# Gates computed between the values' projection steps, and the output gate's projection spread over the steps of the heads' chain, in a two-stage transformer kernel on one core

## The reference

```python
def odd_mixer(nc, nl, w_in, gate_b, head_g, w_out, need_ctx):
    pc = nc @ (w_in if need_ctx else w_in[:, :ML_QKVG])
    pl = nl @ w_in                       # q, k, v, gates, output gate
    qc, kc, vc, gc = mlstm_inputs(pc, gate_b)
    ql, kl, vl, gl = mlstm_inputs(pl, gate_b)
    ...                                  # scans forward and backward: h_l
    h = rmsnorm(h, head_g.reshape(ML_HEADS, ML_DV)).reshape(Bh, T, ML_MIX)
    return (jax.nn.sigmoid(p[..., ML_QKVG:]) * h) @ w_out
```

## Time and profile before

| what | us |
|---|---|
| three runs: median (lowest to highest) | 3825.74 (3823.3 to 3829.73) |
| profiled execution: its own time | 3827.59 |
| its span in the trace | 3826.3 |
| PE busy over the span | 3038.8 (79%) |
| DVE busy over the span | 2461.3 (64%) |
| ACT busy over the span | 762.1 (20%) |
| POOL busy over the span | 930.9 (24%) |

### The profile page before, as it was taken

The page is one execution under the profiler, slowest core; times in us unless marked ns, Lnnn a source line. Parts: engine busy times, 40 slices in busy tenths (PEclk is TensorE's granted clock), DMA queues, the critical chain, the costliest instruction groups (busy, mean ns, idle before and its releaser), DMA issues. The chain is left out here.

```text
span 3826.3 us, 28525 instructions
## 1 busy us (share of the span) xinstructions
PE 3038.8 (79%) x8761; PEld 1590.9 (42%) x8761; DVE 2461.3 (64%) x5376; ACT 762.1 (20%) x1854; POOL 930.9 (24%) x842
## 2 busy tenths in 40 slices
PE   6898886799997889887767778777897786778776
PEld 1354455467433468354344223222343462223222
DVE  2124357798676678745568998666514549997665
ACT  1002123224222523225311111000102211110000
POOL 0000001222322133222302434333100013435332
PEclk7899887899998899988878999999996699999999
DMA  6554334799897579966747999999632059999998
GB/s 221 190 187 152 121 113 147 296 370 351 319 377 284 211 310 414 401 241 212 290 151 281 387 389 397 422 422 421 258 138 103 17 200 357 387 386 415 422 422 341
DMA packets 205546, 1102.17 MB, mean 288 GB/s; under 512 B 23796, under 2 KB 24128, under 8 KB 107088
## 3 DMA queue, kind: packets, MB, share of 16 engines
q0 software_dynamic: 114512, 818.87, 54.0%
q1 hardware_dynamic: 90256, 280.91, 20.4%
q10 hardware_dynamic: 624, 0.57, 0.1%
HBM read 1099.18 MB, written 1.05 MB: 288 GB/s over the span
## 5 line engine op out<-in xcount | busy, mean ns | idle before, releaser
L2098 PE MATMUL PS<-AR 128*128 128x512 f32 x2456 | 1198.5, 633 | 386.1 <-DVE AR L2140 342.7
L2197 POOL DMA_INDIRECT AR<-in_uv,AR x768 | 854.2, 1112 | 1695.2 <-PE PS L2098 1159.5
L2145 DVE CUSTOM_DVE_ANT_0 AR<-AR 128x1024 f32<-128x1024 f32 x768 | 937.3, 1222 | 318.0 <-DMA AR<-in_uv,AR 316.2
L2098 PEld LDWEIGHTS PS<-AR 128*128 128x128 f32 x2456 | 469.4, 200 | 1076.2 <-DVE AR L2140 534.6
L750 PE MATMUL PS<-AR 128*128 128x512 f32 (+4 forms) x1176 | 500.5, 579 | 20.8 <-DMA AR<-in_w_in 6.5
L2110 ACT ACTIVATE AR<-AR 128x2 f32<-128x2 f32 x384 | 78.1, 203 | 1552.7 <-DVE AR L2145 1547.2
L750 PEld LDWEIGHTS PS<-AR 128*128 128x128 f32 x1176 | 222.1, 203 | 279.2 <-issue 243.6
L350 DVE SCALAR_TENSOR_TENSOR AR<-AR,CC 128x512 f32<-128x512 f32 x280 | 211.6, 756 | 184.4 <-DMA AR<-in_w_ada 105.2
L1051 PE MATMUL PS<-AR 128*128 128x256 f32 x1408 | 317.1, 384 | 10.2 <-DMA AR<-in_w_up_lin 8.8
L1051 PEld LDWEIGHTS PS<-AR 128*128 128x128 f32 x1408 | 268.9, 192 | 69.0 <-issue 18.0
L2017 PE MATMUL PS<-AR 128*128 128x256 f32 x768 | 196.3, 420 | 39.7 <-ACT AR L806 19.2
(11 more groups left out here) (226 smaller groups left out, 2578.3 us busy)
## 6 DMA issues: line engine op xcount, KB each, us to landing
AR<-in_w_mod SPq DMA_DIRECT2D x96, 512.0 KB
AR<-in_w_ada SPq DMA_DIRECT2D x160, 256.0 KB, 7.0
AR<-in_w_in SPq DMA_DIRECT2D x56, 512.0 KB
AR<-in_peer_w_q SPq DMA_DIRECT2D x48, 512.0 KB
AR<-in_w_up_act SPq DMA_DIRECT2D x44, 512.0 KB
AR<-in_w_up_lin SPq DMA_DIRECT2D x44, 512.0 KB
AR<-in_w_down SPq DMA_DIRECT2D x44, 512.0 KB
AR<-in_even_w_in SPq DMA_DIRECT2D x24, 512.0 KB
```

Source lines behind the costliest of these rows:

```text
L2098: ins = pe.eng.matmul(acc[i][hh], e.dg(x), e.buf(x)[:, 1024 + 512 * hh:1536 + 512 * hh], start=(x == e.on[False][i][0]), stop=(x == e.on[F ...
L2145: v.eng.tensor_tensor_reduce(e.buf(x)[:, 0:1024], e.buf(x)[:, 0:1024], norm2(e).H[e.tiles[x // 128]], 1.0, 0.0, ALU.mult, ALU.add, DT[x // ...
L2197: g.eng.indirect_dma_start(e.buf(x), None, D["uv"][e.l], bass.IndirectOffsetOnAxis(ap=idx_at(x // 16, x % 16, 1), axis=0)).then_inc(*land. ...
```

## The change

The order becomes `oq`, `ok`, `og`, `ov`, `oo`. In the first four, `odd_front` does two pieces of modulation after each step, and in `ov` one step of the gates as well, on each engine. The projection `oo` is no longer in the front: `odd_units` does one of its eight steps after each iteration of the heads' chain, on PE and ACT. It uses banks 0 and 1 (`GATED`) and the chain's own ring shrinks to banks 2 to 5 (`MID`). The transposes of q and k become a stage of their own, s0, one iteration ahead, so the chain has 12 iterations; the copy of k (`KTO`) moves from DVE to ACT. Since the turned activations must live until `oo` ends, the chain's tiles move from `HT8` to `SL`, behind its first 4096 columns. SP issues the same loads in the new order: two pieces of modulation behind each chunk of the first 17, then the eight chunks of `oo` alone.

```diff
-        EB = [HT8[:, 1536 + 512 * i:2048 + 512 * i] for i in range(6)]
+        EB = [SL[:, 5632 + 512 * i:6144 + 512 * i] for i in range(6)]
...
-        odd_lins = [("oq", (0, 512), [0, 1]), ("ok", (512, 1024), FOUR), ("ov", (1024, 2048), FOUR),
-                    ("og", (2048, 2064), FOUR), ("oo", (2064, 3088), [0, 1])]
+        odd_lins = [("oq", (0, 512), [0, 1]), ("ok", (512, 1024), FOUR), ("og", (2048, 2064), FOUR),
+                    ("ov", (1024, 2048), FOUR), ("oo", (2064, 3088), [0, 1])]
+        GATED, MID = (0, 1), (2, 3, 4, 5)
+
+        def odd_front(lane, steps, gates):
+
+            gates = iter(gates)
+            for n, cols, tiles in odd_lins[:-1]:
+                for _ in steps(n, cols, tiles):
+                    lane.fill(2)
+                    if n == "ov":
+                        next(gates, None)
+            lane.flush()
+            through(gates)
+
+        def odd_units(last, *parts):
+
+            for _ in stages(8, *parts):
+                next(last, None)
+            through(last)
...
+            def gates():
+                for _ in range(4):
+                    yield
+                bk = bank(pe, MAIN, "cum")
+                pe.wait_ge(("lf",), ("late",))
...
+                ins.then_inc(*pe.done("mm", "cum"))
+                yield
+                yield
+                bk = bank(pe, MAIN, "ut")
...
-                    bk = bank(pe, SIX, "ou", u, d)
+                    bk = bank(pe, MID, "ou", u, d)
...
-            skewed(8, s1, nothing, s2, s3)
+            odd_units(steps(*odd_lins[-1]), s0, s1, nothing, s2, s3)
...
+            odd_front(sp, lambda n, cols, tiles: lin(sp, 8, cols, tiles, nothing), ())
+            through(lin(sp, 8, odd_lins[-1][1], [0, 1], nothing))
...
+            def gates():
+                yield
+                a.wait_ge(a.last, ("gl",))
+                a.eng.activation(EG, LG, ACT.Exp, scale=-1.0).then_inc(*a.done("ge"))
+                yield
+                a.wait_ge(a.last, ("g1",))
+                a.eng.activation(EG, EG, ACT.Ln).then_inc(*a.done("gn"))
...
+                    copy_act(a, KTO[h % 2], psum("flip", "ok", h), ("mm", "flip", "ok", h),
+                             ("mm", "osc", u - 3)).then_inc(*a.done("ev", "flip", "ok", h))
...
-                if t == 0:
-                    copy_dve(v, KTO[h % 2], psum("flip", "ok", h), ("mm", "flip", "ok", h),
-                             ("mm", "osc", u - 3)).then_inc(*v.done("ev", "flip", "ok", h))
```

More of the change, by code:

```diff
@@ L2221, in odd_pe @@
             seen = {}
[L2222 to L2239, removed]
+            def steps(n, cols, tiles):
+                return lin_pe(pe, (n,), W3, 8, cols, tiles, ALL.tile, prep=n1, seen=seen,
+                              ring=LINES if n in ("oq", "ok") else GATED if n == "oo" else MAIN)
@@ new lines, in gates @@
+            def gates():
[3 more added lines that the diff above has]
+                pe.wait_ge(("lf",), ("late",))
+                for d, order, tri in ((0, (2, 3, 0, 1), "up"), (1, (3, 2, 1, 0), "lo")):
+                    for n, j in enumerate(order):
+                        for m in range(n + 1):
+                            ins = pe.eng.matmul(bk[:, j * 8 + d * 4:j * 8 + d * 4 + 4], cst(tri) if m == n else cst("one"),
+                                                LG[:, order[m], d * 8 + 4:d * 8 + 8], start=(m == 0), stop=(m == n))
+                ins.then_inc(*pe.done("mm", "cum"))
+                yield
+                yield
+                bk = bank(pe, MAIN, "ut")
+                pe.wait_ge(("ug",))
+                for t in FOUR:
+                    ins = pe.eng.transpose(bk[0:8, t * 128:(t + 1) * 128], UG[:, t, :], ident)
+                ins.then_inc(*pe.done("mm", "ut"))
@@ L2241, in s1, with s0 @@
+            odd_front(pe, steps, gates())
+            def s0(u):
+                h, t = units3[u]
+                if t == 0:
+                    flip_pe(pe, ("oq", h), [Qp[:, i, h * 128:(h + 1) * 128] for i in range(2)], MID,
+                            [("ev", "lin", "oq", x, 0) for x in range(2)])
+                    flip_pe(pe, ("ok", h), [Kp[:, i, h * 128:(h + 1) * 128] for i in FOUR], MID,
+                            [("ev", "lin", "ok", x, 512) for x in FOUR])
             def s1(u):
@@ L2259, in s2 @@
             def s2(u):
-                bk = bank(pe, SIX, "opt", u)
+                bk = bank(pe, MID, "opt", u)
                 pe.wait_ge(("oe", u))
@@ L2309, in odd_act, with steps, s0 @@
             seen = set()
-            for n, cols, tiles in odd_lins:
-                for _ in lin(a, 8, cols, tiles, takes[n], prep=n1, seen=seen):
-                    a.fill()
-            a.flush()
-            a.wait_ge(a.last, ("gl",))
-            a.eng.activation(EG, LG, ACT.Exp, scale=-1.0).then_inc(*a.done("ge"))
-            a.wait_ge(a.last, ("g1",))
-            a.eng.activation(EG, EG, ACT.Ln).then_inc(*a.done("gn"))
-            def s1(u):
+            def steps(n, cols, tiles):
+                return lin(a, 8, cols, tiles, takes[n], prep=n1, seen=seen)
+            def gates():
[5 more added lines that the diff above has]
+                a.eng.activation(EG, EG, ACT.Ln).then_inc(*a.done("gn"))
+            odd_front(a, steps, gates())
+            def s0(u):
                 h, t = units3[u]
@@ L2379, in odd_dve, with steps @@
[L2379 to L2386 removed]
+            def steps(n, cols, tiles):
+                return lin(v, 8, cols, tiles, nothing, prep=n1, seen=seen)
```

79 lines of the change are left out of this document (37 added, 42 removed).

## The result

The change makes the kernel faster. In the runs made beside each other, before took 3827.73 us (3823.3 to 3833.93, 4 runs) and after 3782.32 us (3775.84 to 3786.57, 4 runs): ratio 0.9882, 95% interval 0.9864 to 0.9899, 45.4 us less. The forecast was 3774 in a range of 3758 to 3796.

A forecast was written before the change was run, and what follows sets the result against it. PE bounds the front; a loop of waits, mostly at low clock, bounds the chain. First scores 40.9 us earlier plus 10.6 off the chain save 51.5: span 3774.8, forecast 3774 us, range 3758 to 3796.

The forecast's parts named there:

- The bound of the front: Front, projections before the heads' chain: PE is the limit, nearly always at full clock, busy 107.3 of 111 us.
- my 9.3: Front, within v's steps: the gates' sums 7.1 us, slow matmuls behind 1.7, transposes 0.5; together 9.3 us.
- The loads wait 3 us: Front, q's steps: three loads pass four buffers, costing PE between no wait and 8 us; taken as 3.
- DVE's two pieces (3.1 us) are too: Front, k's and v's steps: DVE's two modulation pieces, 3.1 us, are hidden behind a 7.4 us step.
- The third rival: Front held: four buffers at upper bound (+5 us), gates' round trips bare (+8), giving 3787 us; chance 9%.
- The hand-over to the chain: Front's end: PE waits about 1.8 us for v's copies, six transposes 0.82, first `oo` step 3.7.
- the 2844.98 from which I added up: Front: the old kernel's end of q, k, v and three modulation halves, 2844.98 us, used as base for added work.
- The chain: Heads' chain: 92.5 us for 103.1 with `oo` inside, about 10.0 us an iteration, mean clock over 0.8.
- The first rival: Front and chain: the low clock takes over from v's last steps, 22.5 us slower, 3848 us; chance 4%.
- The added wait: Chain, `oo`'s fifth step: PE waits 5.5 us for ACT to empty banks 0 and 1; iteration 17 us for 10.
- The k copy: Chain: k's copy leaves DVE's loop, where it held every head's first scores; gain counted within the loop's 9.0 us.
- All later stages shifted alike: After the chain: a sign that the forecast is right is that every later stage moves by the same amount.

The follow-up runs named there:

- act_late: after with, on ACT alone, one piece of modulation moved from q's last step to k's first, behind q's copies; median 3774.08 us, ratio 0.9874.
- sig_first: after with ACT's copies and Sigmoids of `oo` ahead of its part of the units within an iteration, PE's list unchanged; median 3777.8 us, ratio 0.9882.
- k_dve_late: gates_only with transposes of q and k back in the iteration that uses them and k's copy back on DVE; median 3815.36 us, ratio 0.9964.
- gates_only: after with `oo` back ahead of the chain, gates and modulation still between the front's projection steps; median 3802.47 us, ratio 0.9939.
- idle_mm: gates_only plus four matmuls of `oo`'s shape, results unread, in eight steps of the chain; median 3802.56 us, ratio 0.9934.
- q_light: after with, on all engines, one piece of modulation beside each step of q and three beside each of k; median 3771.48 us, ratio 0.986.
- both: after with the edits of q_light and sig_first together; median 3769.75 us, ratio 0.9869.

## Why the prediction was right, and where it was off

The time missed by 8.3 us (3782.3 for 3774), and the front alone accounts for it: 160.4 us from its first matmul to the first scores, where my terms gave 2885.9 - 2734.05 = 151.9. That the profiled span, 3774.5, meets the sum's 3774.8 is luck: 6.7 of the 51.8 us saved there are the earlier start, ahead of the change.

- **The bound of the front.** Right: PE without a pause for 122.9 us, gates inside, no wait on them. Their sums took 5.9 us from 2846.24, the transposes 0.6, and the v matmuls behind cost 2 more (16.06 us for 32 records, 14.00 elsewhere): 8.5 for my 9.3.
- **The loads wait 3 us.** Mis-sized by little: 4.5, inside the bounds of 0 to 8.
- **"DVE's two pieces (3.1 us) are too"**, hidden. This is the step that failed. I asked whether DVE's work on two pieces fits beside a step, and it does, though in q DVE also waits for their loads. I did not ask what stands behind them: the norm's last tile comes later, ACT's copy of the first modulation half waits for it, and q's copies stand behind that copy. 6.8 us of wait and 1.8 of slow matmuls; act_late takes 9.1 us off by moving one entry of ACT's list. The third rival had the kind ("every wait stands in an engine's one list"), and put it at the gates, where PE did not wait.
- **The hand-over to the chain.** 2.5 us for 1.8, and the first `oo` step 5.4 for 3.7, at a fallen clock.
- **Waits that my starting point already held.** These misses add up to more than the front's 8.5 us: 1.5 for the loads, 8.6 at q's copies, 2.4 at the hand-over, less 0.8 at the gates, 11.7 together. Most of the rest is that the 2844.98 from which I added up holds 3.7 us of waits of PE for ACT's copies, which I took over unseen; after has none of them but the one at q's copies, and that is in its 6.82 already. That the front missed by 8.5 and not by 12 is luck. Timeline of before, PE:

```profile
2749.78 1.95 PE L750 MATMUL PS<-AR 128*128 128x512 f32 x4 [0.79 <-ACT AR L2303]
...
2782.51 29.43 PE L750 MATMUL PS<-AR 128*128 128x512 f32 x64 [1.36 <-ACT AR L2303]
...
2815.43 27.70 PE L750 MATMUL PS<-AR 128*128 128x512 f32 x64 [1.58 <-ACT AR L2303]
```

- **The chain.** 92.2 for 92.5. First to third scores 15.9 (16.5), third to eighth 56.7 (57), tail 19.7 (19). Four gaps of 8.9 to 12.5, mean 10.05, for my 10. The clock was 0.87, "over 0.8". The first rival, that the low clock takes over, did not come near.
- **The added wait.** 5.63 us for 5.5, that iteration 16.5 for 17. sig_first shows that its cause is the order on ACT, as reckoned.
- **The k copy.** I put its gain into the loop and gave it no size. Without `oo` in the chain, at a clock of 0.65, it is 7.3 us (k_dve_late against gates_only), and it needs only one of the two moves. If it were as much in after, two thirds of the chain's 11.0 us would have nothing to do with `oo` or the clock; no run takes the move back with `oo` in the chain. That the total came out right hides that I had not separated the two.
- **All later stages shifted alike.** Right: 794.5 for 796.3, and 794.4 to 795.7 in all kernels but k_dve_late (798.1).

The prediction weighed the rule of the Trainium skill ("TensorE: Matmul & The Clock Gate", Part 1) that the clock follows how busy PE is. In after, PE was busy 11.83 of 11.90 us from 2903.6 to 2915.5 and the clock granted was 0.57 on the mean:

```profile
2903.60:2915.50 11.90, 11.83 (x18) 4.58 (x19) 6.88 (x22) 2.62 (x6) 0.00 (x0) 0.57 0.05 18
```

So the trace again disagrees with it as a rule on busy time, 8-row spreads and transposes counting as busy. It agrees in so far as idle_mm, with more full matmuls and fewer waits, has the higher clock.

## What to carry to other kernels

When more work is put ahead of an entry in one engine's list, follow not only who waits for that entry but what stands behind those who wait: here four more pieces of modulation ahead of the norm's last tile delayed DVE, then POOL, then ACT's next copy, and with it two copies that had nothing to do with them. An added wait that the profile names "<-ACT" can be a matter of the order on ACT alone, and a small reordering (7.7 and 9.1 us of a section here) is worth trying before the work is moved elsewhere. And undo a change's small companions one by one and together: two moves that each look free can be two cures of the same wait.

## What the runs showed of the hardware

- Matmuls that nobody needs shortened a stretch by 8.0 us, by the clock they kept (0.92 for 0.64).
- The same wait of 2.27 us at the same place was followed by a stretch at 1.2 GHz of different length: q_light's chain has the same lists as after's and takes 9.2 us there for 12.5, and both's has sig_first's and takes 12.5 for 9.2. No edit explains these 3.3 us. They go with an earlier step: the longer stretch came in the traces whose first `oo` step, behind a wait of 2.5 us, had taken 5.37 us and not 3.67. What decides between the two stays open.
- ACT's two table loads (1.28 us each) lengthened no gap between scores in sig_first (8.8 and 9.3 us), though the second puts off an Exp by its length; and in after the Sigmoid starts at 2925.75, straight behind the load from 2924.46.
